# Low-rank products placed behind two projections, and expert weights loaded in 8 KB runs

## The chip, the cores and the metric

The kernel runs on one core of a Trainium2 chip. The metric is the device time of one execution in microseconds: three runs of the kernel before gave 2464.87, 2464.70 and 2462.36 us, median 2464.7 us.

## The reference, cut to what matters

The reference runs 512 tokens of width 1024 through two transformer blocks in float32. Two of its parts matter here.

In the first block, an RWKV-7 mixer projects the normed input to r, k and v (each 1024 wide) and to three low-rank streams. Two of these, of width 64 each, go through a second small product:

```python
w_log = -jax.nn.softplus(-(w0 + jnp.tanh(w_low) @ w2)) - 0.5
decay = jnp.exp(-jnp.exp(w_log))
a = jax.nn.sigmoid(a0 + a_low @ a2)
k_mod = k * (1.0 + (a - 1.0) * k_a)
kk = k * k_k ; kk = kk / max(sqrt(sum(kk * kk)), 1e-12)   # per head
```

The state recurrence over time that follows is computed in chunks of 64 tokens.

The second block ends with a mixture of 32 experts, two per token; every expert's three weight matrices are 1 MB each:

```python
a = einsum('td,edf->tef', t, w_gate)      # w_gate, w_up: [32, 1024, 256]
u = einsum('td,edf->tef', t, w_up)
hid = silu(a) * u * combine[..., None]
y = y + einsum('tef,efd->td', hid, w_down)   # w_down: [32, 256, 1024]
```

The sum over d (1024) in the first two products is where the layout of the weights in memory and that of the tokens have to agree.

## The kernel before, in words

Every engine runs its own program, written out by hand; semaphores alone order them. SyncE (`sp`) issues nearly all loads, in the order of the code, into a ring of four 1 MB buffers (`ring`), for the experts also into `arena`. TensorE takes an ordinary load with `slot()`, and a projection is `half(...)`: 8 matmuls of 128x512 over the 1024 inputs, each of which the chip executes in two passes, so that one half is 16 records in the trace.

**The quads.** The RWKV part goes over four quads, q = 0 to 3, of 256 channels each. A quad has two streams s = 0, 1 of 128 channels. Its order on TensorE: the low-rank products (`lora`, L772 and L773, two per stream, into PSUM banks 4 to 7), then six projection halves (`projected`, L654, banks 0 to 3 in turn), with `ssq` (L789) behind the third of them and `bonus` (L796) behind the sixth, then `tv`, `tat` and further chunk products (L761). Each named product goes through `product(...)`, which waits until the product before the previous one on the same banks has been read.

ScalarE in a quad: four sigmoids of the low-rank products (L1447, L1449), then the scalings of projections 0 and 1 (L1456), then six exponentials (L1464 to L1466), which need VectorE's running sums, then the scaling of projection 2 and the square roots of `ssq` (L1470). VectorE in a quad: for both streams the running sum of the first sigmoid (L2033) and a difference (L2034); then for each stream the shift of a projection (L2002, `add_previous`) and two operations (L2039, L2040) whose end lets `ssq` run (semaphore `chan`); then, from the square root on (L2046), a long serial list that ends with L2069, for which `tat` waits. All engines run their lists strictly in this order.

Ahead of quad 0 two further projections make the inputs of the low-rank products (`LOW`), and ScalarE turns them with tanh and sigmoid (L1423 to L1428); the last of these raises `lora_ready`. TensorE waits for it, and for banks 0 to 2 (`drain_psum`), ahead of quad 0.

**The experts.** Experts go in pairs, 16 pairs in one round of 64 tokens per expert (`expert_pair`). For a pair TensorE does, in order: gate products (L1339, first 32 matmul records), up products (L1339, next 32), the gathering of the tokens of the next pair (L1314, two halves of the width), two transposes of the hidden values (L1347), `turn_tokens` for both halves (L1322, four transposes each, with the gathered tokens as the weights of the transpose), and the down products (L1360). ScalarE copies each gathered half from PSUM to `TOK` (L1825, `tok_copied`), and each turned half to `XE` (L1829), from which the next pair's gate and up products read.

One set of six 1 MB buffers (`EXPERT_W`) holds the weights of a pair; pair 1 alone has a second set (`SECOND_W`). SyncE issues the loads at L602: the gate weights of the next pair when this pair's gate products are done (`gu_done`), up likewise, down when the down products are done (`down_made`). So each buffer has one pair's time, less its own use, to be filled again. The loads view a weight as `(k p)`: partition p gets rows p, 128 + p, 256 + p and so on. A row of gate or up weights is 256 floats (1 KB), a row of down weights 1024 floats (4 KB). The results of each pair, 0.5 MB, are written to DRAM by ScalarE's queue (L1852).

Of the kernel before, what the change touches and what calls it, by code (L numbers as in the profile page):

```python
# [19 lines left out]
P = 128  # L20
T = 512
D = 1024
KT = D // P
# [126 lines left out]
def build(nc, a, stop=99):  # L150

    with ExitStack() as ctx:
# [137 lines left out]
        TOK = area(36864, 2, 512)  # L290
# [106 lines left out]
        def drain_psum(pe, phase):  # L397

            for e in "AD":
                if BEFORE[phase][e]:  # L400
                    pe.wait_ge(freed[e], BEFORE[phase][e])
# [63 lines left out]
        def _(sp):  # L465
# [127 lines left out]
            if stop < 6:  # L593
                return

            gv = a["w_gate_2"].rearrange("e (k p) f -> p e k f", p=P)
            uv = a["w_up_2"].rearrange("e (k p) f -> p e k f", p=P)
            wd = a["w_down_2"].rearrange("e (k p) d -> p e k d", p=P)
            PARTS = ((0, gv, 256), (1, uv, 256), (2, wd, D))

# [39 lines left out]
        def _(pe):  # L640
            n = [0]

            def slot():
                m = n[0]
                n[0] += 1
                pe.wait_ge(full[m % R], full_value(m))
                return m

            def half(m, hf, bank, rhs, width=P, kts=KT, out=None, start=True, stop=True, inc=1, cols_=256, slot_=None):

                w = ring[:, m % R, 0:kts * cols_].rearrange("p (k c) -> p k c", c=cols_)
                dst = ps[0:width, bank, :] if out is None else out
                for k in range(kts):
                    mm = pe.matmul(dst, w[:, k, hf * P:hf * P + width], rhs(k),  # L654
                                   start=(start and k == 0), stop=(stop and k == kts - 1))
                mm.then_inc(half_done, inc)
# [71 lines left out]
            half(m, 0, 2, h_, width=32, cols_=32, inc=2)  # L728


            pe.wait_ge(lora_ready, 1)
            pe.wait_ge(got_lora, 32)
            made_n = [0]

            def product(q, name, s, body, dep=()):
# [27 lines left out]
                return mm  # L763

            for q in range(4):
                if q == 0:
                    drain_psum(pe, "rkv")
                for s in range(2):
                    j = 2 * q + s

# [1 line left out]
                        pe.matmul(ps[:, A, :], W2A2[0:64, j * P:j * P + P], LOW[0:64, :], start=True, stop=True)  # L772
                        return pe.matmul(ps[:, B, :], W2A2[64:128, j * P:j * P + P], LOW[64:128, :], start=True, stop=True)  # L773
                    product(q, "lora", s, lora)

                def projected(m, hf, i):
                    hh = q * 6 + i
                    if hh >= 4:
                        pe.wait_ge(freed["D"], BEFORE["rkv"]["D"] + hh - 3)
                    half(m, hf, hh % 4, h_)  # L780

                m = slot()
                projected(m, 0, 0)
                projected(m, 1, 1)
                m = slot()
                projected(m, 0, 2)
                for s in range(2):
# [521 lines left out]
            def gather(value, par, hf):  # L1309
# [5 lines left out]
                                       start=(tt == 0 and i_ == 0), stop=(tt == 3 and i_ == 1))  # L1315
                mm.then_inc(gathered, 1)

            def turn_tokens(value, hf):

                pe.wait_ge(tok_copied, value)  # L1320
                for k in range(4):
                    mm = pe.transpose(ps[:, TOK_BANK[hf], k * P:k * P + P], TOK[:, hf, k * P:k * P + P], ident)  # L1322
                mm.then_inc(tok_turned, 1)

            for hf in range(2):
                pe.wait_ge(h2_low, 4 * hf + 4)
                gather(2, 0, hf)
            for hf in range(2):
                turn_tokens(hf + 1, hf)

            def expert_pair(pair, j, weights, full_, loaded):
                pe.wait_ge(xe_ready, pair * 2 + 2)
                for part in range(2):
                    for k in range(KT):
                        for e in range(2):
                            if k == 0:
                                pe.wait_ge(full_[2 * part + e], loaded)
                            w = weights[2 * part + e].rearrange("p (k c) -> p k c", c=256)
                            mm = pe.matmul(ps[e * SLOTS:(e + 1) * SLOTS, 2 + part, 0:256],  # L1339
                                           XE[:, j, k, e * SLOTS:(e + 1) * SLOTS], w[:, k, :],  # L1340
                                           start=(k == 0), stop=(k == KT - 1))
                    mm.then_inc(gu_done, 1)
                gather(pair * 2 + 4, 1 - j, 0)
                gather(pair * 2 + 4, 1 - j, 1)
                pe.wait_ge(mhid, pair + 1)
                for f in range(2):
                    mm = pe.transpose(ps[:, 6, f * P:f * P + P], MH[:, f * P:f * P + P], ident)  # L1347
                mm.then_inc(hid_turned, 1)
                turn_tokens(pair * 2 + 3, 0)
                turn_tokens(pair * 2 + 4, 1)  # L1350
                pe.wait_ge(hid_ready, pair + 1)
                pe.wait_ge(copied["A"], pair + 1)
                pe.wait_ge(copied["D"], pair + 1)
                for e in range(2):
                    pe.wait_ge(full_[4 + e], loaded)
                for c in range(2):
                    for f in range(2):
                        for e in range(2):
                            w = weights[4 + e].rearrange("p (k c) -> p k c", c=D)
                            mm = pe.matmul(ps[e * SLOTS:(e + 1) * SLOTS, 4 + c, :], MHT[:, f, e * SLOTS:(e + 1) * SLOTS],  # L1360
                                           w[:, f, c * 512:c * 512 + 512], start=(f == 0), stop=(f == 1))
                mm.then_inc(down_made, 1)
# [1283 lines left out]
```

## Time and profile before

| | |
|---|---|
| median of three runs | 2464.7 us |
| profiled execution | 2460.87 us, its span 2459.1 us |
| TensorE busy | 2225.8 us, 91% of the span |
| mean granted TensorE clock | 0.958 |
| moved by DMA | 295.24 MB, mean 120 GB/s |
| DMA rate in the slices 2213 to 2398 us | 369 GB/s in each of three slices |

How to read it: TensorE is busy nearly everywhere, so the place to look is the chain of waits, which names what TensorE stood for when it stood still. The granted clock is a fraction of 2.4 GHz. The mean DMA rate hides two regimes: for most of the span the queues are nearly idle, and in the last tenth they are busy without a break.

### The profile page before, as it was taken

What the parts mean: (1) busy time and instruction counts of PE and PEld (TensorE: products, weight loads), DVE (VectorE), ACT (ScalarE), POOL (GpSimd) and SP (SyncE); (2) the same over time, 40 slices, a digit from 0 to 9 for tenths busy, and PEclk for the clock granted to TensorE, in tenths of its full rate; (3) what the DMA queues carried; (4) which work ended last, traced back from release to release, by engine and by line L of the source; (5) the groups of instructions that cost most, each with busy time, mean ns of one, the idle gap of its engine ahead of it and who ended that gap; (6) DMA issues with size and microseconds to landing.
All of it is one profiled execution on the core that took longest, in us unless ns stands there. A gap on an engine that the chain in (4) does not pass through costs nothing.

```text
span 2459.1 us, 41070 instructions
## 1 busy us (share of the span) xinstructions
PE 2225.8 (91%) x17656; PEld 1568.0 (64%) x17656; DVE 1125.6 (46%) x1999; ACT 728.0 (30%) x1095; POOL 217.1 (9%) x97
## 2 busy tenths in 40 slices
PE   7989999999989999888899998977899998898984
PEld 5385959594437889664378876856555686555552
DVE  4546454544666565344267771253355634411113
ACT  2323232311431222352333331251244523322221
POOL 0020202020000000000133433400000000000001
PEclk9999999998989999999999999988999999899997
DMA  7201010104447555003233322244120234699994
GB/s 249 78 11 53 4 52 4 52 8 127 137 146 228 187 180 156 26 1 103 69 86 85 102 81 82 94 78 123 31 77 18 69 93 137 211 304 369 369 369 150
DMA packets 273657, 295.24 MB, mean 120 GB/s; under 512 B 7640, under 2 KB 257408, under 8 KB 273504
## 3 DMA queue, kind: packets, MB, share of 16 engines
q1 hardware_dynamic: 268128, 274.85, 35.0%
q0 software_dynamic: 3072, 9.74, 1.9%
q10 hardware_dynamic: 2304, 8.39, 0.8%
q8 instruction: 124, 2.03, 0.3%
q14 instruction: 29, 0.24, 0.0%
HBM read 279.84 MB, written 13.11 MB: 119 GB/s over the span
## 4 chain that ended last, share of the span: by engine, by line
PE 73%; DVE 10%; DMA 6%; ACT 4%; issue 2%; another core or an unknown queue 2%; SPq 1%; POOL 1%; POOLq 0%; DVEq 0%; ACTq 0%
PE ps L654 11%; PE ps L1132 10%; PE ps L761 9%; PE ps L982 7%; PE ps L950 5%; PE ps L1161 5%; DMA ring<-in_w_up 4%; PE ps L1339 4%; PE ps L1006 3%; PE ps L1036 2%; PE ps L1052 2%; PE ps L1314 2%; DVE arena L2202 1%; PE ps L1064 1%
## 5 line engine op out<-in xcount | busy, mean ns | idle before, releaser
L761 PE MATMUL ps<-arena 64*64 64x64 f32 x7168 | 226.3, 222 | 14.4 <-POOL arena L1875 8.8
L761 PEld LDWEIGHTS ps<-arena 64*64 64x64 f32 x7168 | 221.8, 138 | 18.5 <-POOL arena L1875 9.6
L654 PE MATMUL ps<-hT,ring 128*128 128x512 f32 (+1 forms) x480 | 212.3, 600 | 3.1 <-ACT hT L1412 2.4
L1881 POOL TENSOR_TENSOR w_low<-ring,w_high 128x2048 fp32r<-128x2048 f32 x22 | 101.2, 4601 | 837.1 <-ACT w_high L1638 837.1
L654 PEld LDWEIGHTS ps<-hT,ring 128*128 128x128 f32 (+1 forms) x480 | 90.4, 190 | 122.0 <-issue 119.5
L654 PE MATMUL ps<-arena,ring 128*128 128x512 f32 (+1 forms) x336 | 150.4, 605 | 12.4 <-DVE arena L2396 6.4
L1132 PE MATMUL ps<-h_high,w_low 128*128 128x512 f32 x352 | 140.3, 399 | 7.8 <-DVE h_low L2278 7.8
L1132 PE MATMUL ps<-h_high,w_high 128*128 128x512 f32 x352 | 140.3, 399 | 0.0
L1132 PE MATMUL ps<-h_low,w_high 128*128 128x512 f32 x352 | 139.0, 395 | 0.0
L1339 PE MATMUL ps<-ring,arena 128*64 128x256 f32 x960 | 119.0, 397 | 21.6 <-DMA ring<-in_w_up 20.9
L654 PEld LDWEIGHTS ps<-arena,ring 128*128 128x128 f32 (+1 forms) x336 | 63.0, 189 | 96.7 <-issue 82.7
L1438 ACT ACTIVATE arena<-ps 128x512 f32<-128x512 f32 x104 | 62.1, 597 | 210.2 <-PE ps L761 199.9
L2202 DVE CUSTOM_DVE_ANT_0 arena<-ps,arena 128x256 f32<-128x256 f32 (+3 forms) x160 | 67.0, 468 | 124.2 <-PE ps L1052 124.1
L1339 PEld LDWEIGHTS ps<-ring,arena 128*64 128x64 f32 x960 | 80.2, 143 | 63.8 <-DMA ring<-in_w_up 25.2
L2019 DVE TENSOR_TENSOR arena<-ps,arena 128x512 f32<-128x512 f32 x88 | 60.9, 692 | 117.2 <-PE ps L761 117.0
L2300 DVE TENSOR_TENSOR rstd<-arena 128x512 f32<-128x512 f32 x22 | 98.4, 4475 | 17.4 <-ACT arena L1678 17.4
L982 PE MATMUL ps<-h_high,w_low 128*128 128x512 f32 x256 | 102.7, 401 | 3.6 <-issue 3.6
L982 PE MATMUL ps<-h_low,w_high 128*128 128x512 f32 x256 | 101.8, 398 | 0.0
L982 PE MATMUL ps<-h_high,w_high 128*128 128x512 f32 x256 | 101.7, 397 | 0.0
L1596 ACT ACTIVATE arena<-arena,small 128x384 f32<-128x384 f32 (+6 forms) x96 | 68.0, 708 | 110.7 <-DVE small L2210 110.7
L1875 POOL TENSOR_TENSOR arena<-arena,const 128x512 f32<-128x512 f32 x40 | 49.6, 1270 | 471.3 <-DVE arena L2015 447.8
L1954 DVE SCALAR_TENSOR_TENSOR arena<-arena,small 128x256 f32<-128x256 f32 x168 | 81.4, 485 | 15.1 <-DMA arena<-in_w_ada 9.6
(400 smaller groups left out, 4281.9 us busy)
## 6 DMA issues: line engine op xcount, KB each, us to landing
ring<-in_w_in SPq DMA_DIRECT2D x54, 1024.0 KB, 5.3
arena<-in_w_ada SPq DMA_DIRECT2D x80, 512.0 KB, 4.0
arena<-in_w_down SPq DMA_DIRECT2D x32, 1024.0 KB, 9.5
ring<-in_w_gate SPq DMA_DIRECT2D x30, 1024.0 KB, 11.4
ring<-in_w_up SPq DMA_DIRECT2D x30, 1024.0 KB, 11.6
ring<-in_w_up SPq DMA_DIRECT2D x44, 512.0 KB, 4.8
ring<-in_w_down SPq DMA_DIRECT2D x8, 1024.0 KB, 5.1
y_scratch<-arena ACTq DMA_DIRECT2D x16, 512.0 KB, 7.2
```

The source lines that it names most:

```text
L654: mm = pe.matmul(dst, w[:, k, hf * P:hf * P + width], rhs(k), start=(start and k == 0), stop=(stop and k == kts - 1))
L761: mm = pe.matmul(ps[r, bank, cc], l[r, cc], x[r, 0:64] if x is eye64 else x[r, cc], start=(i == 0), stop=(i == len(terms) - 1))
L950: mm = pe.matmul(ps[:, bank, :], w_[:, k, hf * P:hf * P + P], x_, start=(k == 0 and i_ == 0), stop=(k == n_ - 1 and i_ == 2))
L982: mm = pe.matmul(ps[:, bank, :], w_[:, k, hf * P:hf * P + P], x_[:, k, :], start=(k == 0 and i_ == 0), stop=(k == KT - 1 and i_ == 2))
L1006: mm = pe.matmul(ps[:, hh % 4, tt * 256:tt * 256 + 256], x_[:, k, tok:tok + P], w_[:, k, :], start=(k == 0 and i_ == 0), stop=(k == KT - 1 ...
L1132: mm = pe.matmul(ps[:, (2 * (m - first) + g) % 4, :], w_[:, k, :], x_[:, k, :], start=(k == 0 and i_ == 0), stop=(k == KT - 1 and i_ == 2))
L1161: mm = pe.matmul(ps[:, hh % 4, :], w_[:, k, hf * P:hf * P + P], x_, start=(kt == 0 and i_ == 0), stop=(kt == FT - 1 and i_ == 2))
L1339: mm = pe.matmul(ps[e * SLOTS:(e + 1) * SLOTS, 2 + part, 0:256], XE[:, j, k, e * SLOTS:(e + 1) * SLOTS], w[:, k, :], start=(k == 0), stop= ...
L1881: pool.tensor_tensor(W_LOW[:, slot_, :], ring[:, slot_, :], W_HIGH[:, j % 2, :].bitcast(F32), ALU.subtract).then_inc(w_low, 1)
L1954: ins = stt(ACC[:, j % 5, :], w[:, k, :], c[k], ACC[:, j % 5, :], ALU.mult, ALU.add)
L2202: dve.tensor_tensor_reduce(out=prob[i % 2][e][:, at:at + mask.shape[1]], in0=out, in1=mask, scale=1.0, scalar=NEG, op0=ALU.add, op1=ALU.ma ...
L2300: tt(val, sil[:, jj % 2, :], cvt[jj % 2][1], ALU.mult).then_inc(dve_link, 1)
```

## The change

Two parts that have nothing to do with each other.

1. In each quad the low-rank products move behind the first two projection halves. The wait for `lora_ready` and `got_lora` goes with them in quad 0, and the common wait for banks 0 to 2 ahead of quad 0 (`drain_psum(pe, "rkv")`) becomes three waits, one at the first projection into each bank.
2. The gate and up weights are viewed as `(p k)`: partition p gets rows 8p to 8p + 7, which lie together in memory (8 KB). So that the products still sum matching pairs, the tokens are turned in the same order: chunk k of a turn takes columns k, 8 + k, 16 + k and so on of `TOK`, across both halves, a step of eight floats. Each turn therefore waits until both halves have been copied (`turn_tokens(2, hf)`, `turn_tokens(pair * 2 + 4, 0)`). The down weights keep their layout.

```diff
-            gv = a["w_gate_2"].rearrange("e (k p) f -> p e k f", p=P)
-            uv = a["w_up_2"].rearrange("e (k p) f -> p e k f", p=P)
+            gv = a["w_gate_2"].rearrange("e (p k) f -> p e k f", p=P)
+            uv = a["w_up_2"].rearrange("e (p k) f -> p e k f", p=P)
...
-            pe.wait_ge(lora_ready, 1)
-            pe.wait_ge(got_lora, 32)
             made_n = [0]
...
             for q in range(4):
+                def projected(m, hf, i):
+                    hh = q * 6 + i
+                    if hh >= 4:
+                        pe.wait_ge(freed["D"], BEFORE["rkv"]["D"] + hh - 3)
+                    elif hh < 3:
+                        pe.wait_ge(freed["D"], BEFORE["lora"]["D"] + hh + 1)
+                    half(m, hf, hh % 4, h_)
+
+                m = slot()
+                projected(m, 0, 0)
+                projected(m, 1, 1)
                 if q == 0:
-                    drain_psum(pe, "rkv")
+                    pe.wait_ge(lora_ready, 1)
+                    pe.wait_ge(got_lora, 32)
                 for s in range(2):
...
                     product(q, "lora", s, lora)
-
-                def projected(m, hf, i):
-                    hh = q * 6 + i
-                    if hh >= 4:
-                        pe.wait_ge(freed["D"], BEFORE["rkv"]["D"] + hh - 3)
-                    half(m, hf, hh % 4, h_)
-
-                m = slot()
-                projected(m, 0, 0)
-                projected(m, 1, 1)
                 m = slot()
                 projected(m, 0, 2)
...
+            tok_rows = TOK.rearrange("s h c -> s (h c)").rearrange("s (p k) -> s k p", k=KT)
+
             def turn_tokens(value, hf):
 
                 pe.wait_ge(tok_copied, value)
                 for k in range(4):
-                    mm = pe.transpose(ps[:, TOK_BANK[hf], k * P:k * P + P], TOK[:, hf, k * P:k * P + P], ident)
+                    mm = pe.transpose(ps[:, TOK_BANK[hf], k * P:k * P + P], tok_rows[:, hf * 4 + k, :], ident)
                 mm.then_inc(tok_turned, 1)
...
-                turn_tokens(hf + 1, hf)
+                turn_tokens(2, hf)
...
-                turn_tokens(pair * 2 + 3, 0)
+                turn_tokens(pair * 2 + 4, 0)
                 turn_tokens(pair * 2 + 4, 1)
```

TensorE at the start of quad 0, before. `32x512` is the last of the projections that feed the low-rank products, L772 and L773 are these products, `full` says that a ring buffer has landed, `freed_by_dve` that a bank has been read.

```order
L654 MATMUL ps<-hT,ring 32x512 x7
L772 MATMUL ps<-arena 128x512 [waits freed_by_dve,got_lora,lora_ready]
L773 MATMUL ps<-arena 128x512
L772 MATMUL ps<-arena 128x512
L773 MATMUL ps<-arena 128x512
L654 MATMUL ps<-hT,ring 128x512 [waits full1]
L654 MATMUL ps<-hT,ring 128x512 x15
L654 MATMUL ps<-hT,ring 128x512 [waits full2]
L654 MATMUL ps<-hT,ring 128x512 x7
L789 MATMUL ps<-arena,const 128x512 [waits emptied_by_act,chan_ready] x2
```

TensorE at the same place, now; the low-rank products are L782 and L783 of the changed file.

```order
L654 MATMUL ps<-hT,ring 32x512 x7
L654 MATMUL ps<-hT,ring 128x512 [waits freed_by_dve,full1]
L654 MATMUL ps<-hT,ring 128x512 x7
L654 MATMUL ps<-hT,ring 128x512 [waits freed_by_dve]
L654 MATMUL ps<-hT,ring 128x512 x7
L782 MATMUL ps<-arena 128x512 [waits got_lora,lora_ready]
L783 MATMUL ps<-arena 128x512
L782 MATMUL ps<-arena 128x512
L783 MATMUL ps<-arena 128x512
L654 MATMUL ps<-hT,ring 128x512 [waits freed_by_dve,full2]
L654 MATMUL ps<-hT,ring 128x512 x7
L789 MATMUL ps<-arena,const 128x512 [waits emptied_by_act,chan_ready] x2
```

Sixteen matmuls have moved ahead of the four low-rank ones, and eight instead of 24 stand between these and L789. The three other quads change in the same way, without the waits for `got_lora` and `lora_ready`.

SyncE's first loads of expert weights, before.

```order
L602 DMA ring<-in_w_gate 128x8x256 x2
L602 DMA ring<-in_w_up 128x8x256 x2
L602 DMA arena<-in_w_down 128x2x1024 x2
L602 DMA arena<-in_w_gate 128x8x256 x2
L602 DMA arena<-in_w_up 128x8x256 x2
L602 DMA arena<-in_w_down 128x2x1024 x2
```

The same loads, now.

```order
L602 DMA ring<-in_w_gate 128x2048 x2
L602 DMA ring<-in_w_up 128x2048 x2
L602 DMA arena<-in_w_down 128x2x1024 x2
L602 DMA arena<-in_w_gate 128x2048 x2
L602 DMA arena<-in_w_up 128x2048 x2
L602 DMA arena<-in_w_down 128x2x1024 x2
```

The order of the loads has not moved; of gate and up weights each partition's share is now one run of 2048 floats instead of eight of 256.

## Rows read from the trace of the kernel before

**Rows 1.** The page's chain that ended last: share of the span by engine.

```profile
PE 73%; DVE 10%; DMA 6%; ACT 4%; issue 2%; another core or an unknown queue 2%; SPq 1%; POOL 1%; POOLq 0%; DVEq 0%; ACTq 0%
```

**Rows 2.** Chain of waits, expert pairs: start us, us, what.

```profile
2156.89 6.91 PE ps L1339 x64
...
2172.58 7.10 PE ps L1339 x64
...
2182.57 13.94 DMA ring<-in_w_up
...
2410.38 0.70 DVE arena L2572
```

**Rows 3.** Windows: PE, PEld, DVE, ACT, POOL busy; PEclk, DMA share, GB/s.

```profile
2202.00:2210.00 8.00, 7.97 (x40) 4.95 (x42) 0.79 (x2) 2.39 (x4) 0.00 (x0) 1.00 1.10 348
2194.00:2198.00 4.00, 1.45 (x12) 0.89 (x14) 0.00 (x0) 0.00 (x0) 0.00 (x0) 0.92 1.03 419
...
2232.00:2236.00 4.00, 2.39 (x18) 1.56 (x20) 0.00 (x0) 0.00 (x0) 0.00 (x0) 0.86 1.03 421
```

**Rows 4.** DMA view, 2202 to 2210, then 2194 to 2198.

```profile
DMA packets 2767, 2.79 MB, mean 348 GB/s; under 512 B 47, under 2 KB 2767, under 8 KB 2767
...
DMA packets 465, 1.67 MB, mean 419 GB/s; under 512 B 33, under 2 KB 64, under 8 KB 465
```

**Rows 5.** DMA issues, 2160 to 2402: count, KB each, us to landing.

```profile
ring<-in_w_gate SPq DMA_DIRECT2D x26, 1024.0 KB, 11.4
...
y_scratch<-arena ACTq DMA_DIRECT2D x13, 512.0 KB, 7.2
```

**Rows 6.** Timeline in pair 0: TensorE's weight loads of the turns, ScalarE's copy.

```profile
2136.22 0.47 PEld L1322 LDWEIGHTS ps<-const,arena 128*128 128x128 f32 x4
2136.95 0.42 PEld L1322 LDWEIGHTS ps<-const,arena 128*128 128x128 f32 x4 [0.27 <-ACT arena L1825]
...
2136.31 0.60 ACT L1825 ACTIVATE arena<-ps 128x512 f32<-128x512 f32 x1 [1.22 <-PE ps L1314]
```

**Rows 7.** Timeline of TensorE, quads 0 and 1: start us, us.

```profile
72.99 0.69 PE L772 MATMUL ps<-arena 64*128 64x512 f32 x1 [4.08 <-ACT small L1428]
...
75.48 21.95 PE L654 MATMUL ps<-hT,ring 128*128 128x512 f32 x48
...
126.53 8.42 PE L761 MATMUL ps<-const,arena 64*64 64x64 f32 x192 [3.04 <-DVE arena L2069]
...
194.80 0.69 PE L772 MATMUL ps<-arena 64*128 64x512 f32 x1
...
196.72 20.87 PE L654 MATMUL ps<-hT,ring 128*128 128x512 f32 x48
...
246.69 5.82 PE L761 MATMUL ps<-const,arena 64*64 64x64 f32 x192 [3.05 <-DVE arena L2069]
```

**Rows 8.** Timeline of ScalarE, quad 1.

```profile
199.35 0.69 ACT L1449 ACTIVATE arena<-ps,cols 128x512 f32<-128x512 f32 x1
...
210.75 0.78 ACT L1456 ACTIVATE arena<-ps,small 128x512 f32<-128x512 f32 x1 [6.09 <-PE ps L654]
211.55 1.28 ACT L1464 ACT_TABLE_LOAD   x1
...
215.46 0.61 ACT L1466 ACTIVATE arena<-arena 128x512 f32<-128x512 f32 x1
...
219.71 1.26 ACT L1470 ACTIVATE arena<-ps,small 128x512 f32<-128x512 f32 x2
```

**Rows 9.** Timeline of VectorE, quad 1.

```profile
198.78 1.23 DVE L2033 TENSOR_TENSOR_SCAN arena<-const,arena 128x512 f32<-128x512 f32 x1 [6.45 <-ACT arena L1449]
...
204.70 0.75 DVE L2002 SCALAR_TENSOR_TENSOR arena<-ps,cols,arena 128x511 f32<-128x511 f32 x1 [2.11 <-ACT arena L1456]
...
206.01 0.69 DVE L2040 TENSOR_TENSOR arena<-arena 128x512 f32<-128x512 f32 x1
...
220.43 0.43 DVE L2046 TENSOR_SCALAR arena<-arena 128x512 f32<-128x512 f32 x1 [1.25 <-ACT arena L1470]
```

## The prediction, made before the changed kernel ran

> **What bounds the kernel now.** I read the page's chain first, then the chain of waits in order of time where it leaves TensorE, then windows of the DMA rate, then the timelines of single engines around the two places that the change touches. The page's chain is TensorE for 73% of the span, VectorE for 10%, DMA for 6% [rows 1]. So a DMA can be worth up to 6% somewhere, and VectorE matters where TensorE waits for it.
>
> The DMA share sits in the experts. Pair 2 starts its gate products at 2156.89 and pair 3 at 2172.58: 15.69 us a pair, TensorE alone being the limit. From then on the chain runs through loads of up weights, the first of them for 13.94 us, and the last of pairs 3 to 15 ends its down products at 2410.38 [rows 2]. That is 237.8 us for 13 pairs, 18.29 us each, 2.6 more than TensorE needs. What limits them is the rate of the queues. Where only packets of 1 KB run (all 2767 under 2 KB) the rate is 348 GB/s; where they are nearly all 4 KB (down weights and results; 64 of 465 under 2 KB) it is 419, and 421 in a second window [rows 3, 4]. With 1.049 MB a load and 0.524 MB of results a pair [rows 5]: gate and up, four loads, 4.194 MB at 348 = 12.05 us; down 2.097 MB at 419 = 5.0; results 1.25. Sum 18.3 us, which is the measured 18.29. The queues explain the pair by themselves.
>
> In the quads TensorE waits twice for others: 4.08 us ahead of the low-rank products of quad 0, for the small ScalarE operation that raises `lora_ready`, and 3.04 and 3.05 us ahead of `tat` for VectorE's L2069, in quads 0 and 1 [rows 7]; I take the other two quads to be like quad 1. VectorE's list from L2046 at 220.43 to L2069 is serial, so `tat` starts when that list started plus its length. L2046 itself waited for ScalarE's square root [rows 9].
>
> **Part 1a, 8 KB runs: the DMA side.** A partition's share becomes one run of 8 KB. No row shows this size in a saturated stretch. Bounds: the 348 of 1 KB packets below (nothing gained), and above a further step from 419 of a few per cent, say 430, as an estimate. I take the nearest row, the 4 KB one, 419 to 421, as 420. Gate and up: 4.194 / 420 = 10.0 us instead of 12.05. A pair needs 10.0 + 5.0 + 1.25 = 16.25 us of the queues.
>
> The same rows show a load rate over what a page would allow: the Trainium skill, HBM Reference, section Specifications (TRN2), gives about 358 GB/s as one core's effective share. By that ceiling gate and up would take 11.7 us, and the result would be near no gain; but the 419 and 421 lie above it, so the trace disagrees, and the page itself says that a core streaming alone goes higher.
>
> **Part 1b, 8 KB runs: TensorE's side.** The turn of the first half used to run while ScalarE copied the second (copy at 2136.31, 0.60 us): its four weight loads start at 2136.22 and last 0.47 us, those of the second half start at 2136.95 behind a wait for that copy [rows 6]. Now both stand behind the copy: + 0.44 us a pair, with nothing to cover it. Behind the waiting turn stand only the down products and the next pair's gate products on TensorE; DMA waits for those in turn.
>
> The transposes now load their weights with a step of eight floats. No row shows a weight load with a step. Bounds: 0 extra, since the loads (0.47 us for four, 0.11 each [rows 6]) may stay hidden beside the previous transpose, and a doubling, 8 x 0.11 = 0.88 us a pair. I take 0.2, nearer to the row as it stands. TensorE then needs 15.69 + 0.44 + 0.2 = 16.3 us a pair, as much as the queues. With two limits so close, each will now and then wait for the other; I take 16.4.
>
> The page that speaks against this is the Trainium skill, SBUF — State Buffer, section Door 1: The DMA port swizzle: SBUF has lines of 16 bytes, so that float32 operands step freely up to four elements, and each access to a new line pays. A step of eight would pay on every element. No run here shows it; it is the reason for the first rival below.
>
> Sum of part 1: pair 3's start moves later by four turns (that of the start and those of pairs 0 to 2) of 0.64 us = 2.6, to 2175.2. Thirteen pairs of 16.4 = 213.2 end at 2388.4 instead of 2410.38: **-22.0 us**. The bounds: 16.25 a pair and only 0.44 a turn, 2172.6 + 1.8 + 211.2 = 2385.6, -24.8; with 430 GB/s TensorE's 16.13 is the limit, -26; with doubled weight loads 17.0 a pair and 1.32 a turn, 2172.6 + 5.3 + 221.0 = 2398.9, -11.5. The three early pairs have no other loss, since their weights are there.
>
> **Part 2, low-rank products behind two projections.** In quad 0 TensorE no longer stands for `lora_ready`: at 13.7 us of projections (two thirds of 20.8) the flag is long up. That removes 4.08 us. But the later place delays ScalarE, which takes the sigmoids ahead of the scalings. Counted from 194.80, where quad 1 now starts with projections, each step by its row:
> - two projection halves, two thirds of 20.87 less the overlap at their end: 13.7, low-rank products from 208.5;
> - sigmoids end as long behind them as before (194.80 to 200.04): 213.8 [rows 7, 8];
> - two scalings of 0.78, then table load and six exponentials (211.55 to 216.07, 4.5), the third scaling 0.8, a table load 1.3, and 0.7 from the square root's start to L2046: 13.8 + 1.5 + 4.5 + 0.8 + 1.3 + 0.7 [rows 8, 9] gives 222.5.
>
> L2046 started at 220.43, so VectorE's serial list, and with it `tat`, comes **2.0 us later** in every quad. VectorE itself is ready: two running sums and two differences (2 x (1.23 + 0.69) = 3.8 from about 212.5), then 2.0 for each stream's shift and two operations (204.70 to 206.70), so `chan` of stream 1 comes at 220.3 [rows 9]. `ssq` of TensorE, which stood at 217.6 (196.72 + 20.87), now stands for that until 220.3, and the later three halves end at 220.3 + 0.9 + 20.8 = 242.0, just ahead of the shift that wants them. So the new wait (about 1.2 us for stream 0 and 1 for stream 1) eats TensorE's lead, not the end. Nothing hides the 2.0, for VectorE has no gap between L2046 and L2069.
>
> Quads 1 to 3: 3 x 2.0 = +6.0. Quad 0: -4.1 of the wait, +2.0, and the first projections no longer run at a lowered clock after it (48 matmuls in 21.95 against 20.87 us, and the low-rank products some 0.6 slower [rows 7]): -1.7. **Sum +2.2 us.** Bounds: -5.8 if the 2.0 is hidden everywhere, and +6.6 if each of the four new waits costs the 1.1 us that a lowered clock cost those 48 matmuls. The chunk products behind the wait ahead of `tat` took 8.42 us in quad 0 and 5.82 in quad 1 [rows 7]; this spread of 2.6 us a quad is there before and after and may fall either way. The single waits for banks cost nothing: the first projection needs bank 0 alone, and the sigmoids behind `lora_ready` (72.99) already wait for the readers of all three.
>
> **Sum.** -22.0 + 2.2 = -19.8 us on the profiled execution's 2460.87 (its span is 2459.1) = 2441.1. The median of the runs is 3.8 above that execution: **2445 us**.
>
> **The rivals.** About 0.2% or 4.9 us is what a measurement of this kernel can tell from no change.
> 1. *Stepped weight loads cost double.* For it: the page above. Against it: the 0.11 us a transpose may be set by the moving side. Then TensorE is the limit at 17.0 a pair, as worked out: -11.5 + 2.2, on the median 2455.4.
> 2. *The rate doesn't rise.* 8 KB runs stay at 348. For it: nothing but the missing row; against it: 419 with 4 KB. Pairs stay at 18.3, the queues start 3 x 0.64 later: +1.9 + 2.2, 2468.8, no change by the bound.
> 3. *Slower: the stepped weight loads become the bound of the expert stage.* If each transposing load costs d more, part 1 ends 4 x (0.44 + 8d) + 13 x (16.13 + 8d) after 2172.6. That, with the 2.2 of part 2, reaches the old end at d = 0.18, a transpose of 0.29 instead of 0.11, and is measurably slower from d = 0.21. At 0.5 us a transpose a pair takes 19.25: pair 3 starts 14.2 later, 13 pairs last 250.3, +26.7 + 2.2, about 2494. Against it: so large a factor has no row near it.
> 4. *Part 2 is free or a gain.* VectorE's list may have slack where I see none: -22 to -26 and -5.8, 2434 to 2437.
>
> **Chances.** Forecast (2437 to 2451): 0.62. Rival 1 (2451 to 2460): 0.22. Rival 4: 0.07. Rival 2: 0.05. Rival 3: 0.04. Below the 2459.8 that counts as faster lie the forecast and rivals 1 and 4: 0.91; same 0.05; slower 0.04. The range, from between rival 4 and the forecast to most of rival 1: 2436 to 2458.
>
> **What would show it.** In the chain of waits from 2180 on: loads of up weights nearly gone, pairs 16.2 to 16.6 apart; over 17 with no DMA in the chain is rival 1. In the DMA windows: gate and up weights at 410 to 430 GB/s. In the group of the turning transposes: weight loads of 0.14 us and a pace of 0.11 say that the step is free; a pace over 0.2 says rival 1, over 0.3 rival 3. TensorE's waits for the copy of the second half should grow to some 0.7 us a pair. In the quads: no wait for `lora_ready`, two waits ahead of `ssq`, L2046 some 2.0 us later counted from the quad's start, `tat` with it, and the distance from one quad's first matmul to its `tat` 53.9 instead of 51.9 in quad 1. I am wrong if the queues stand idle between pairs while TensorE waits for them (then the single set of buffers, not rate, is the limit), or if the time between `lora` and L2046 shrinks.

## The result, and the profile after

The changed kernel takes 2446.56 us (median of 4 runs, 2444.70 to 2449.29) against 2464.78 us for the kernel before on the same chip (4 runs, 2462.36 to 2468.87): ratio 0.9931, 95% interval 0.9915 to 0.9947, so 18.2 us less (13 to 21). Forecast were 2445.0 us and 19.8 less. The profiled execution took 2447.23 us, its span is 2445.4 us at a mean granted clock of 0.960 (before 2459.1 at 0.958). The two profiles differ by only 13.7 us of the 18.2; how far one profile can be off stands at the end.

The page: the GB/s of the 40 slices, the packets, and the chain that ended last, answering [rows 1].

```profile
GB/s 251 86 4 52 4 53 4 53 4 115 132 169 213 182 168 185 35 1 87 77 78 86 102 87 78 95 75 135 28 91 18 35 103 108 190 291 408 400 404 143
DMA packets 216313, 295.24 MB, mean 121 GB/s; under 512 B 7640, under 2 KB 191872, under 8 KB 207968
...
PE 77%; DVE 8%; DMA 6%; ACT 4%; another core or an unknown queue 2%; issue 2%; SPq 1%; POOL 1%; POOLq 0%; DVEq 0%; ACTq 0%
...
L1341 PE MATMUL ps<-ring,arena 128*64 128x256 f32 x960 | 111.4, 380 | 3.4 <-DMA ring<-in_w_up 2.4
```

The same megabytes move, at 400 to 408 GB/s in the three busy slices of the experts where it was 369. TensorE's gate and up products (L1341, L1339 before) now stand idle for 3.4 us in all, where it was 21.6. The share of DMA in the chain has not fallen: it is 6% as before.

The chain of waits through the expert pairs (start us, us, what), which answers to [rows 2]:

```profile
2162.00 6.91 PE ps L1341 x64
...
2178.18 6.91 PE ps L1341 x64
...
2201.98 13.33 DMA ring<-in_w_up
...
2228.32 6.93 PE ps L1341 x64
...
2235.70 13.64 DMA ring<-in_w_up
...
2262.33 6.93 PE ps L1341 x64
...
2396.76 0.70 DVE arena L2574
```

The early pairs, whose weights are there, are 16.18 us apart (2162.00 to 2178.18) where they were 15.69. From 2178.18 to 2396.76 the other thirteen take 218.6 us, 16.81 each, where they took 18.29. Loads of up weights are still in the chain, each for 12.7 to 13.6 us. Where the chain passes through one, the pair takes 16.9 to 17.8 us (in the first, 0.4 for the issue, 13.33 for the load and 3.67 for the second up products); up to 2295 each such pair is followed by one of 16.2 that TensorE alone sets, later four of them stand in a row.

The DMA view where all but 44 of the packets are of 8 KB (2255 to 2262), and windows around the stretch that follows; columns as in [rows 3]:

```profile
DMA packets 409, 2.99 MB, mean 427 GB/s; under 512 B 44, under 2 KB 44, under 8 KB 44
```

```profile
2260.00:2263.00 3.00, 3.00 (x20) 1.29 (x18) 0.62 (x2) 0.60 (x1) 0.00 (x0) 1.00 1.03 429
2263.00:2268.00 5.00, 5.00 (x49) 3.50 (x47) 0.74 (x3) 1.67 (x2) 0.00 (x0) 1.00 0.92 304
2268.00:2271.00 3.00, 3.00 (x20) 2.12 (x17) 0.42 (x1) 0.00 (x0) 0.00 (x0) 1.00 1.02 419
```

8 KB packets run at 427 to 429 GB/s, a little over the 419 to 421 taken from [rows 3, 4]. But about once in two pairs the rate falls for some 5 us, here to 304. The DMA view of that stretch (2263 to 2268), and SyncE's issues (start us, us) around it:

```profile
DMA packets 354, 1.52 MB, mean 304 GB/s; under 512 B 24, under 2 KB 24, under 8 KB 313
```

```profile
2253.08 0.81 SPq L602 DMA_DIRECT2D ring<-in_w_up  x2
2262.37 0.90 SPq L602 DMA_DIRECT2D arena<-in_w_down  x2
2265.97 1.08 SPq L602 DMA_DIRECT2D ring<-in_w_gate  x2
```

The down load is issued when TensorE's down products of that pair free the buffer. By then the up load, issued 9.3 us earlier, has nearly drained, and the gate load comes 3.6 us later, so in the dip the 4 KB packets of the down load move almost alone (313 of 354 packets are under 8 KB). It is tempting to say that the queues have too little to do. That is not shown: the DMA engines' share falls only from 1.02 or 1.03 to 0.92, while the rate falls by 29%. A dip costs about (429 - 304) x 5 us = 0.6 MB, as an estimate 1.5 us of queue time.

The turn in pair 1, answering to [rows 6], and the group of all turns, duration in ns as min/median/max (before, first the weight loads, then the matmuls: 138/140/143 and 270/273/330):

```profile
2140.39 0.60 ACT L1827 ACTIVATE arena<-ps 128x512 f32<-128x512 f32 x1 [1.23 <-PE ps L1314]
...
2141.03 0.97 PEld L1324 LDWEIGHTS ps<-const,arena 128*128 128x128 f32 x8 [0.70 <-ACT arena L1827]
2141.04 1.16 PE L1324 MATMUL ps<-const,arena 128*128 128x128 f32 x8 [0.47 <-ACT arena L1827]
...
L1324 PEld LDWEIGHTS ps<-const,arena x136: 185/193/207, 2127.5 to 2392.7; 128*128 128x128 f32 x136
L1324 PE MATMUL ps<-const,arena x136: 273/276/376, 2127.5 to 2392.9; 128*128 128x128 f32 x136
```

A weight load with a step of eight floats takes 193 ns instead of 140. Eight of them still go through in 0.97 us, 0.12 each, so they overlap; before, four took 0.42 to 0.47. The wait of the loads for the copy is 0.70 us, as the prediction had it.

Quad 1 on TensorE, answering to [rows 7], and the end of the same quad on ScalarE and VectorE, answering to [rows 8, 9]:

```profile
189.15 14.00 PE L654 MATMUL ps<-hT,ring 128*128 128x512 f32 x32
203.08 0.69 PE L782 MATMUL ps<-arena 64*128 64x512 f32 x1
...
212.84 1.13 PE L789 MATMUL ps<-arena,const 128*128 128x512 f32 x2 [0.70 <-DVE arena L2042]
214.74 1.13 PE L789 MATMUL ps<-arena,const 128*128 128x512 f32 x2 [0.78 <-DVE arena L2042]
215.71 20.76 PE L654 MATMUL ps<-hT,ring 128*128 128x512 f32 x48
...
243.25 5.82 PE L759 MATMUL ps<-const,arena 64*64 64x64 f32 x192 [3.05 <-DVE arena L2071]
```

```profile
216.18 1.26 ACT L1472 ACTIVATE arena<-ps,small 128x512 f32<-128x512 f32 x2
```

```profile
216.90 0.43 DVE L2048 TENSOR_SCALAR arena<-arena 128x512 f32<-128x512 f32 x1 [1.25 <-ACT arena L1472]
```

L2048 (L2046 before) starts 216.90 - 189.15 = 27.75 us after the quad's first matmul; before it was 220.43 - 194.80 = 25.63. `tat` starts 54.1 us after it instead of 51.9. In quad 0 the wait for `lora_ready` is gone, the granted clock from 70 to 80 us is 1.00 where it was 0.83, and `tat` starts at 121.53 instead of 126.53.

### The profile page after: what moved, and what is told of

It is laid out like the page before. It is cut to its first block, busy times and chain, and to the rows that moved or that the text cites. A ratio compares the mean times of both kernels' runs of the same rounds, so it can differ in the third digit from the quotient of the medians.

```text
span 2445.4 us, 41058 instructions
## 1 busy us (share of the span) xinstructions
PE 2223.7 (91%) x17656; PEld 1563.0 (64%) x17656; DVE 1125.4 (46%) x1999; ACT 725.1 (30%) x1095; POOL 217.1 (9%) x97
## 4 chain that ended last, share of the span: by engine, by line
PE 77%; DVE 8%; DMA 6%; ACT 4%; another core or an unknown queue 2%; issue 2%; SPq 1%; POOL 1%; POOLq 0%; DVEq 0%; ACTq 0%
PE ps L654 13%; PE ps L1132 10%; PE ps L759 9%; PE ps L982 8%; PE ps L950 6%; PE ps L1161 5%; DMA ring<-in_w_up 4%; PE ps L1341 4%; PE ps L1006 3%; PE ps L1036 2%; PE ps L1052 2%; PE ps L1314 2%; PE ps L1064 2%; PE ps L1188 1%
## 5 line engine op out<-in xcount | busy, mean ns | idle before, releaser
L1341 PE MATMUL ps<-ring,arena 128*64 128x256 f32 x960 | 111.4, 380 | 3.4 <-DMA ring<-in_w_up 2.4
L1341 PEld LDWEIGHTS ps<-ring,arena 128*64 128x64 f32 x960 | 73.1, 137 | 45.0 <-issue 7.7
```

## The experiments

Each kernel is compared with the kernel before on its own chip, whose median stands beside it; those medians differ by up to 8.7 us, so ratios are what to compare. "Sixteen pairs" is the time from the first gather (L1314) of the expert stage to the last one, in one profile of each kernel: 284.7 us before (2116.80 to 2401.49), 267.0 in the changed kernel (2120.36 to 2387.34).

| kernel | median, before's, us | ratio, 95% interval | sixteen pairs, us |
|---|---|---|---|
| changed kernel | 2446.56, 2464.78 | 0.9931, 0.9915 to 0.9947 | 267.0 |
| low-rank part alone | 2468.08, 2464.68 | 1.0015, 0.9998 to 1.0031 | 285.1 |
| 8 KB part alone | 2447.67, 2464.68 | 0.9936, 0.9911 to 0.9961 | 263.8 |
| the same, second time | 2448.54, 2459.47 | 0.9946, 0.9928 to 0.9964 | 265.5 |
| 8 KB, low-rank moved in quad 0 only | 2447.12, 2464.68 | 0.9916, 0.9885 to 0.9947 | 268.1 |
| 8 KB, plain turn, late | 2448.92, 2459.47 | 0.9959, 0.9945 to 0.9973 | 268.6 |
| 8 KB, plain turn, early | 2442.11, 2468.14 | 0.9895, 0.9870 to 0.9920 | 260.4 |
| 8 KB, step of four, early | 2440.82, 2459.47 | 0.9912, 0.9884 to 0.9940 | 263.8 |
| 1 KB, step of eight, late | 2465.97, 2468.14 | 0.9992, 0.9980 to 1.0003 | 287.5 |
| two 4 KB, step of four, early | 2438.67, 2468.14 | 0.9880, 0.9856 to 0.9903 | 262.9 |
| two 4 KB, step of four, early, low-rank moved in quad 0 only | 2437.05, 2464.68 | 0.9885, 0.9860 to 0.9910 | 263.0 |
| two 4 KB, step of four, late, low-rank moved in quad 0 only | 2439.80, 2468.14 | 0.9900, 0.9876 to 0.9925 | 265.3 |

"Late" means that both turns wait for both token copies; "early", each half for its own. Four of these kernels (the three with 8 KB runs and a turn other than the changed kernel's, and the one with 1 KB runs) do not turn the tokens in the order of the weight rows, so their products sum rows with other tokens; the operations and their sizes are the same, and only the time is read from them.

**The two parts apart.** First the low-rank products alone, then the 8 KB runs alone. The edit of the first, against the changed kernel:

```diff
-            gv = a["w_gate_2"].rearrange("e (p k) f -> p e k f", p=P)
-            uv = a["w_up_2"].rearrange("e (p k) f -> p e k f", p=P)
+            gv = a["w_gate_2"].rearrange("e (k p) f -> p e k f", p=P)
+            uv = a["w_up_2"].rearrange("e (k p) f -> p e k f", p=P)
```

The turn goes back to its old order, and to each half's own copy, with it. The second is the kernel before with part 2 of the change alone.

> Only the low-rank products moved in all four quads, expert loads and turns as before. Theory (the gain is the experts', the move costs VectorE's list 2 us a quad and saves about 6 in quad 0): 0 to +5 us against before, about 2467. Rival (the wait for the flag was the gain, the later sigmoids are covered): 4 to 8 us faster, about 2459. In the profile: two short waits ahead of ssq and the square root's reader 2 us later, counted from each quad's first matmul.

Measured: 2468.08 us (12 runs), 3.4 us over the kernel before, interval -0.5 to +7.6. The predicted +2.2 lies in it, and so does nothing at all; a gain of 5.8 doesn't.

> Only the 8 KB runs and the stepped turns, quads as before. Theory: all of the gain, 18 to 24 us faster than before, about 2443 to 2446, pairs 17.0 us apart from pair 4 on and 16.2 ahead of it. Rival (both parts share the gain): only 10 to 14 us faster.

Measured: 2447.67 us (7 runs), 17.0 less, 1 us short of what was expected. The same code measured once more (at the end of this section) gave 10.9 less, so the size is not known to better than some us; but with the low-rank part alone giving no gain, the gain of the change is the runs'. Thirteen pairs from pair 3 on took 16.57 us each here, not the 17.0 expected.

**The low-rank part kept where it helps.** In quad 0 the low-rank products stand behind the first projection half; in quads 1 to 3 where they stood before. With 8 KB runs:

```diff
+                if q == 0:
+                    m = slot()
+                    projected(m, 0, 0)
+                    pe.wait_ge(lora_ready, 1)
+                    pe.wait_ge(got_lora, 32)
                 for s in range(2):
                     ...
-                m = slot()
-                projected(m, 0, 0)
+                if q:
+                    m = slot()
+                    projected(m, 0, 0)
                 projected(m, 1, 1)
```

> 8 KB runs as in the changed kernel; the low-rank products stand behind one projection half in quad 0 and ahead of all of them in quads 1 to 3, as before. Theory: keeps the 5 to 6 us of the flag's wait in quad 0 without the 2 us a quad, so 5 to 6 us below runs only and 6 to 8 us below the changed kernel, about 2439. Rival (the 2 us a quad are not real and only the clock moved): equal to the changed kernel within 2 us.

Measured: 2447.12 us, ratio 0.9916: the forecast of 2439 missed, and by the total the rival (no difference) holds. `tat` of quad 3 starts at 479.64 where the changed kernel has 485.38 (before 483.85). One mark in two profiles can differ by as much on unchanged code (below), but here more profiles are on record. In the three kernels with this edit `tat` of quad 3 starts at 477.27 to 481.75 (mean 479.6), in the eight with the old order, the kernel before among them, at 483.13 to 489.07 (mean 484.7), and in the two with all quads moved at 485.38 and 489.37. So the edit is worth some 5 us up to that mark, which is 0.2% of the total and less than the intervals can tell.

**Two 4 KB runs instead of one of 8 KB.** Each half of the rows is spread over the partitions for itself, so a turn needs only its own half of the tokens, with a step of four floats:

```diff
-            gv = a["w_gate_2"].rearrange("e (p k) f -> p e k f", p=P)
+            gv = a["w_gate_2"].rearrange("e (h p k) f -> p e h (k f)", h=2, p=P)
...
-            PARTS = ((0, gv, 256), (1, uv, 256), (2, wd, D))
+            PARTS = ((0, gv, 4 * 256), (1, uv, 4 * 256), (2, wd, D))
...
-                    mm = pe.transpose(..., tok_rows[:, hf * 4 + k, :], ident)
+                    mm = pe.transpose(..., TOK[:, hf, :].rearrange("s (p k) -> s k p", k=4)[:, k, :], ident)
...
-                turn_tokens(pair * 2 + 4, 0)
+                turn_tokens(pair * 2 + 3, 0)
```

> As quad0_only_runs8, but each partition gets two runs of 4 KB (rows 4p to 4p + 3 of each half of the width), so that a turn needs one half of the tokens alone and steps by four floats. Theory (the rate of the queues is the limit, 4 KB packets move at 420 against 428 GB/s): pairs 0.0 to 0.2 us longer where DMA is the limit, early pairs 15.7 to 15.9 instead of 16.2; total within 2 us of quad0_only_runs8. Rival (TensorE's 0.5 us a pair is what is left to gain): 13 x 0.5 = 6 us faster than it. Weight loads of the turns: 0.14 us if four floats are a free step, 0.19 if not.

Measured: 2437.05 us (6 runs), 27.6 less than before and 10.1 below the kernel with 8 KB runs and the same low-rank order. Neither the theory (within 2 us of it) nor the rival (6 us faster) said as much; the rival, that TensorE's 0.5 us a pair is left to gain, was the nearer. The group of its turns:

```profile
L1326 PEld LDWEIGHTS ps<-const,arena x136: 195/211/219, 2124.7 to 2386.6; 128*128 128x128 f32 x136
L1326 PE MATMUL ps<-const,arena x136: 271/284/387, 2124.9 to 2386.7; 128*128 128x128 f32 x136
```

A step of four makes a load no shorter than one of eight: 211 ns against 193. The early pairs are 15.8 us apart. With the same runs and turns and the old order of the low-rank products:

> Two 4 KB runs per partition with the stepped turn (4 elements), low-rank products where before has them. If quad 0's edit is worth what the traces show at the tat products (2 us earlier in quad 3), 2439 to 2442; the pairs 16.5 to 16.6 us as with that edit.

Measured: 2438.67 us, ratio 0.9880 against 0.9885: in the total, quad 0's edit is within the noise, and the 4 KB runs with their early turn carry the gain. From the sixth on its pairs are 16.54 to 16.56 apart, except the last two (17.93, 16.31), with 412 GB/s over each of the steady ones. They have no dips; around the issue of a down load:

```profile
2259.00:2262.00 3.00, 3.00 (x20) 1.15 (x16) 0.36 (x1) 0.36 (x1) 0.00 (x0) 1.00 1.02 406
2262.00:2267.00 5.00, 4.86 (x46) 2.97 (x42) 1.00 (x3) 1.90 (x3) 0.00 (x0) 1.00 1.03 413
2267.00:2270.00 3.00, 3.00 (x23) 1.91 (x20) 0.42 (x1) 0.00 (x0) 0.00 (x0) 1.00 1.02 415
```

**Is it the packets or the late turn?** The changed kernel's queues are faster while they run and yet its pairs are slower (16.81 against 16.55). Theory Q puts that on the 8 KB packets, theory T (called L further down) on TensorE's later turn. Five kernels bear on it.

The step and the wait at 1 KB runs, where the queues leave TensorE 2.6 us a pair:

> Gate and up rows in the old 1 KB runs, tokens turned in the new stepped order behind both copies (so rows and tokens are paired wrongly, which leaves the output other than the reference's). Both theories: the turn is hidden by the transfers at 1 KB, so a pair takes 18.3 us as before (0 to +0.1) and the time is that of before, -2 to +3. If the step or the wait reached the queues, a pair would be over 18.5 us and the time over +4.

Measured: 2465.97 us, ratio 0.9992; pairs 18.3 to 18.4 apart where steady, sixteen 2.8 us longer than before, of which the three early pairs, where TensorE alone is the limit, make 1.5. Where the queues leave room, the edit costs next to nothing. This fits both theories.

8 KB runs, the turn as it was (old order, each half behind its own copy):

```diff
-                turn_tokens(2, hf)
+                turn_tokens(hf + 1, hf)
...
-                turn_tokens(pair * 2 + 4, 0)
+                turn_tokens(pair * 2 + 3, 0)
```

> Gate and up rows in 8 KB runs, tokens turned in the old order and each half behind its own copy (rows and tokens are paired wrongly, the output is not the reference's). Theory Q (what makes the later pairs 17.0 us is the queues with 8 KB packets: the dip in the rate of each pair): pairs stay 16.8 to 17.1 us from the fifth on and the time is within 3 us of the same kernel with the stepped turn (2447.67 then). Theory T (TensorE's later turn issues the next loads later): pairs fall to 16.3 to 16.6 us and the time to 2438 to 2443.

Measured: 2442.11 us, ratio 0.9895, against 0.9936 and 0.9946 for the late stepped turn. Sixteen pairs 260.4 us, the fifth 17.91, from the sixth on 16.04 to 16.74 and 16.36 in the mean. This is what T forecast, and not what Q did.

The 4 KB kernel with a late turn:

> The kernel with two 4 KB runs and low-rank products moved in quad 0 alone (2437.05 then), its turns made to wait for both token copies. Theory Q: pairs stay 16.5 to 16.6 us, time within 2 us of 2437. Theory T: pairs 16.9 to 17.1 us, time 2443 to 2446.

Measured: 2439.80 us, ratio 0.9900 against 0.9885 and 0.9880, pairs from the sixth on 16.5 to 16.6 but for three: Q's figure for the pairs, its time missed by 0.8 us (on a chip whose kernel before is 3.5 us slower). Here the late turn is nearly hidden. At 412 GB/s the queues need 16.55 a pair, TensorE 16.27 even with the late turn; at 8 KB it is about 16.36, the mean with the early turn, against 16.2. So neither theory is whole. That it is the closeness of the two limits that counts fits all these kernels; no run varies it alone.

8 KB, old order of the turn, but behind both copies; then the early turn with a step of four:

> 8 KB runs, tokens turned in the old order (rows paired with the wrong tokens), but behind both token copies. Early pairs 16.1 (15.69 + 0.44). Theory L (the late turn takes away TensorE's slack against queues that need 16.35 a pair): the sixteen pairs together take 263 to 267 us, as with the stepped late turn (263.8, 267.0 and 268.1 in three profiles), against 260.4 with the early turn. Rival S (the stepped weight load does it): 260 to 262 us.

> 8 KB runs, each half turned behind its own copy with a step of 4 elements (rows paired with the wrong tokens). Early pairs 15.8 as with two 4 KB runs. Theory L: the sixteen pairs take 260 to 262 us. Rival S: 263 to 267 us.

Measured: plain late 2448.92 us, ratio 0.9959, sixteen pairs 268.6 us, early pairs 16.1; stepped early 2440.82 us, ratio 0.9912, 263.8 us, early pairs 15.8. These two were compared with the same runs of the kernel before, and their intervals do not meet. And the 8 KB part once more, to see what one profile is worth:

> The same instructions as the kernel with 8 KB runs alone (2447.67 then, sixteen pairs 263.8 us): the spread of one profile to the next. Pairs 263 to 268 us, time 2443 to 2450.

Measured: 2448.54 us, 10.9 less than before; sixteen pairs 265.5 us. The same expert code gave 263.8, 265.5, 267.0 and 268.1 us in four profiles, so a profile tells this to some 2 us. The late plain turn (268.6, above even the 267 that L gave) lies with the late ones, and its time's interval is clear of that of the early plain turn: the wait is what costs, at 8 KB some 4.5 us (mean of the five late profiles 266.6, of the two early ones 262.1). About 1.4 of it falls on the three early pairs. What the step adds is not settled: the early stepped turn (263.8) missed L's 260 to 262 and fits S's range, yet with the late turn the step added nothing.

One window, 2200 to 2380, shows PE busy and the rate. Of the changed kernel, of the early plain turn, of the late plain turn, of the 4 KB kernel with the old low-rank order:

```profile
2200.00:2380.00 180.00, 172.15 (x1117) 107.43 (x1113) 22.93 (x52) 41.31 (x69) 0.00 (x0) 1.00 1.01 405
```

```profile
2200.00:2380.00 180.00, 177.32 (x1162) 109.11 (x1160) 24.16 (x55) 44.68 (x72) 0.00 (x0) 1.00 1.01 413
```

```profile
2200.00:2380.00 180.00, 169.21 (x1108) 107.79 (x1108) 22.87 (x53) 41.62 (x70) 0.00 (x0) 1.00 1.00 401
```

```profile
2200.00:2380.00 180.00, 177.41 (x1144) 109.44 (x1142) 23.87 (x55) 43.09 (x70) 0.00 (x0) 1.00 1.03 412
```

It looks as if queues that run dry hold TensorE up. The groups of the turns and of the first products, 2100 to 2430, say what TensorE stood for: first the changed kernel, then the early plain turn (busy us, mean ns, then idle time and what ended it).

```profile
L1324 PE MATMUL ps<-const,arena 128*128 128x128 f32 x136 | 19.7, 288 | 8.2 <-ACT arena L1827 8.2
L1341 PE MATMUL ps<-ring,arena 128*64 128x256 f32 x960 | 111.4, 380 | 3.4 <-DMA ring<-in_w_up 2.4 <-ACT arena L1831 0.7
```

```profile
L1322 PE MATMUL ps<-const,arena 128*128 128x128 f32 x136 | 21.3, 279 | 0.8 <-ACT arena L1825 0.3
L1339 PE MATMUL ps<-ring,arena 128*64 128x256 f32 x960 | 113.1, 380 | 3.1 <-DMA ring<-in_w_up 2.1 <-ACT arena L1829 0.7
```

The waits for the copy differ by 7.4 us, those for up weights by 0.3. In the window the waits for the copy are 5.2 us, which is the whole difference between 172.15 and 177.32. So the idle time seen is the late turn's own wait. How much TensorE waited for weights can't be read from its busy time: the same matmuls count 15.78 us in an early pair of the 4 KB kernel and 16.42 in a steady one.

Nor does the rate belong to the late turn alone. The four profiles of the changed kernel's expert code show 401, 405, 408 and 412 GB/s over this window. The time that the rate is under 350, counted us by us, is 23, 22, 18 and 11 us in these four, in the same order; it is 25 with the late plain turn, 10 and 18 with the early plain and the early stepped turn, and 0 in the 4 KB kernel above (3 and 5 in the two others). The dips are fewer with an early turn, but not gone, and the 4 KB kernel has none though its down load is the same.

## Why the prediction was right

**Queues bound the experts, by their rate.** Right. With longer runs the rate rose from 348 GB/s to 427 and the pairs shrank from 18.29 to 16.81; the 8 KB part alone, measured twice, gave 17.0 and 10.9 us against the 18.2 of both parts. Taking 420 from the 4 KB rows was nearly 2% low. Two of the signs named did not come: loads of up weights hold 4% of the page's chain as before, where they were to be nearly gone, and the pairs are not 16.2 to 16.6 apart. Rival 2 (the rate stays) is out.

**The share of about 358 GB/s** that the Trainium skill gives for one core (HBM Reference, Specifications (TRN2)) was set against 419 in the trace. It is passed by 427 here too. The same section gives about 425 GB/s for a core that streams alone, and with that the trace agrees.

**TensorE's side.** The copy's wait (0.44) and the step (0.2) were taken together as 0.64 a pair; the early pairs show 16.18 against 15.69, 0.5. With the late plain turn they are 16.13 apart: the wait is the 0.44 forecast, and the step, put at 0.2, is some 0.05 to 0.1. Pair 3 starts 57.8 us after the first gather instead of 55.8: +2.0, forecast +2.6. The Trainium skill's rule (SBUF — State Buffer, Door 1: The DMA port swizzle) that float32 steps beyond four elements pay shows in the length of a load, 193 ns for 140. But a step of four, which that rule lets go free, paid more (211 ns); there the measurement decides. The pace of the turn, hidden by the overlap of loads, hardly moved. Rivals 1 and 3, which let the step double or triple the pace, are out.

**The pair's pace.** This is the mis-sized term. 16.4 a pair was max(16.25, 16.3) and a little; measured were 16.81, that is 218.6 us for the thirteen instead of 213.2, 5.4 more. The prediction said that each limit would now and then wait for the other, and priced that at 0.1. With the early plain turn, where TensorE needs only 15.69, the thirteen pairs took 16.42 each, so the queues' side was itself 0.1 to 0.2 above its 16.25. With the late turn the other three profiles of the same expert code show 16.57, 16.70 and 16.89. So the late turn, with TensorE at 16.2, adds another 0.15 to 0.5 a pair, and one profile doesn't tell its size better than that. The explanation offered is that loads are issued when TensorE frees their buffers, so that a late TensorE starts them late, and a pair at 16.2 has no slack to catch up. It fits the kernels with early turns, but is argued: by how much the rate dips are caused by it, no run shows. The prediction had named a single set of buffers as the limit if the queues stood idle between pairs; they do not, their share is 1.01 over 2200 to 2380 and 0.92 in a dip, yet part of the shortfall may be of this kind. That part 1 gave -17.2 in the profile (293.6 us from the first gather to the last down products' reader before, 276.4 after) instead of -22.0 is these 5.4 us less the 0.6 gained at the start.

**Part 2.** +2.2 forecast. The steps inside a quad came as worked out: L2048 2.1 us later (2.0 forecast), `tat` 54.1 us behind the first matmul (53.9), the waits ahead of `ssq` 0.70 and 0.78 us (1.2 and 1), the wait for `lora_ready` gone. `tat` of quad 0 comes 5.0 earlier (3.8 forecast), that of quad 3 1.5 later; against the mean of the eight profiles with the old order, the two with all quads moved are 0.7 and 4.7 later. Alone, the part measured +3.4, -0.5 to +7.6: right in mechanism, and in size not separable from zero. Rival 4, that the delay is hidden, is out by the steps in quad 1.

**The sum.** -17.2 and +1.5 make -15.7; the profiles' span shows -13.7 and the medians -18.2. The 2 us between the first two lie between quad 3 and the experts, where the code did not change: the experts started 3.6 us later, of which 1.5 is part 2. That -19.8 lies so near to -18.2 is partly luck: the pace was 5.4 us too good in this profile, and the parts measured alone (17.0 or 10.9 less, 3.4 more) add up to 7.5 to 13.6 less, not 18.2, though within their noise.

## What to carry to other kernels

Before lengthening the runs of a load, ask what the other layout asks of the consumer: the run length that lets each half of the data be used on its own (4 KB here, ratio 0.9880) beat the longer one (0.9931), at a lower peak rate. What it gained is the early turn: 8 KB runs with an early turn, which leave the products' rows and tokens unmatched, gave 0.9895 and 0.9912. Where two limits come within a few per cent of each other and the loads' issue waits for the consumer (single buffers), price the pair above the larger of the two; here 0.15 to 0.5 us on 16.4. A product moved later on TensorE delays the engines that read it: by the marks in the traces it was worth moving where its flag was late (quad 0, some 5 us) and lost 2.1 us a quad elsewhere, both too little for the total time to show.

## What the runs showed of the hardware

Loads saturating the queues: 348 GB/s with 1 KB packets [rows 4]; 419 over 4 us with nearly all 4 KB [rows 4], 412 over whole pairs of 4 KB; 427 over 7 us with 8 KB, but 401 to 412 over ten pairs with 8 KB gate and up loads and 4 KB down loads behind a late turn.

A weight load from float32 with a step of four or eight elements took 211 and 193 ns against 140 without, and the pace of the transposes stayed within 0.01 to 0.03 us of the 0.11.

The granted clock falls at other moments in each execution: in windows of 10 us from 60 to 500 it is below 1.00 in nine in the kernel before and in thirteen in the kernel with 8 KB runs and the early plain turn. Here is `tat` of quad 3 in the latter, whose code up to this point is that of the kernel before (483.85 us there):

```profile
489.07 7.11 PE L761 MATMUL ps<-const,arena 64*64 64x64 f32 x192 [3.05 <-DVE arena L2069]
```

5.2 us later without any change, and its expert stage began at 2128.38 against 2116.80. The mean clock of 500 to 2100 was 0.96 in both. A difference of under 5 us at one mark in two profiles says nothing; distances within one stage, the same mark in several profiles, and times over several runs, do. Not settled: why the rate dips, and why in one pair and not in the next at equal timing, and why single pairs of 17.8 to 17.9 us turn up in the 4 KB kernels as well, at full granted clock.
